# A decoder layer with routed experts on one core: router turned tile by tile, gates of the experts first, last weights in halves, the samples' delta-rule states computed behind the slot indices

## The reference, cut to what matters

```python
def decoder_layer(x, ...):
    h = rmsnorm(x, norm_mix)
    ... = jnp.split(h @ w_in, points, axis=-1)
    # three branches: mLSTM, gated delta rule (state S, 4 heads of 128 x 128 per sequence), cross-attention
    mixed = (sigmoid(gate_a) * (h_a @ w_br_mlstm) + sigmoid(gate_b) * (h_b @ w_br_gdn)
             + sigmoid(gate_c) * (h_c @ w_br_xattn))
    x = x + mixed @ w_out
    x = x + hier_moe(rmsnorm(x, norm_ffn), ...)     # then one final rmsnorm
def hier_moe(h, ...):
    lg = t @ w_router_group + b                     # 4 groups, the best one
    le = t @ w_router_expert + b                    # the best 2 of its 4 experts
    for gidx in range(4):                           # 16 experts, 1024 -> 512 -> 1024
        a = einsum('td,edf->tef', t, w_exp_gate[e0:e1])
        u = einsum('td,edf->tef', t, w_exp_up[e0:e1])
        out = out + einsum('tef,efd->td', silu(a) * u * comb, w_exp_down[e0:e1])
# delta rule, per chunk: Sm = g_last * Sm + k_dec^T v_new     (returned as gdn_S_sample for the samples)
```

## Time and profile before

| | |
|---|---|
| three runs, median (lowest to highest) | 919.81 us (917.28 to 924.47) |
| the profiled execution, whole | 914.95 us |
| its span, first to last instruction | 913.1 us |
| PE busy | 774.1 us (85%), mean granted clock 0.922 |
| DVE, ACT, POOL busy | 278.2, 151.4, 64.1 us |
| moved by DMA | 189.90 MB, mean 208 GB/s |

### The profile page before, as it was taken

How to read it: one execution, slowest core, us unless ns; L and a number is a source line. 1 busy time by engine, 2 the same in 40 slices (tenths; PEclk the granted TensorE clock), 3 DMA queues, 4 the chain that set the end, 5 groups by cost and what they waited for, 6 DMA issues and landing times. The chain is left out here.

```text
span 913.1 us, 10617 instructions
## 1 busy us (share of the span) xinstructions
PE 774.1 (85%) x4441; PEld 421.5 (46%) x4441; DVE 278.2 (30%) x702; ACT 151.4 (17%) x347; POOL 64.1 (7%) x97
## 2 busy tenths in 40 slices
PE   7999999889884989998897899999799787877760
PEld 3544577654552566555654435455333332332220
DVE  2150134568262442164216441135111110110004
ACT  3112122102331301140113110120000000000012
POOL 3102000003111000000001010002100000000002
PEclk9999999889997799999998879999899989988985
DMA  8956525505624200042204337409599999999934
GB/s 275 345 155 198 155 92 184 196 24 180 265 77 176 73 1 1 1 167 110 93 1 144 122 122 276 185 26 412 184 413 423 425 422 418 427 421 421 420 133 155
DMA packets 48830, 189.90 MB, mean 208 GB/s; under 512 B 5110, under 2 KB 5347, under 8 KB 44682
## 3 DMA queue, kind: packets, MB, share of 16 engines
q1 hardware_dynamic: 38922, 155.54, 43.8%
q0 software_dynamic: 9856, 33.63, 11.1%
HBM read 175.47 MB, written 17.88 MB: 212 GB/s over the span
## 5 line engine op out<-in xcount | busy, mean ns | idle before, releaser
L1148 PE MATMUL PS<-ring,arena 128*64 128x512 f32 x384 | 93.1, 643 | 20.8 <-issue 20.8
L1446 ACT ACTIVATE arena<-PS 128x512 f32<-128x512 f32 (+7 forms) x142 | 58.9, 441 | 268.5 <-PE PS L933 73.7
L864 PE MATMUL PS<-ring,hT 128*128 128x512 f32 x192 | 92.5, 630 | 0.4 <-ACT ring L1446 0.4
L562 PE MATMUL PS<-ring,hT 128*128 128x512 f32 x192 | 86.1, 605 | 0.0
L1148 PEld LDWEIGHTS PS<-ring,arena 128*64 128x64 f32 x384 | 32.9, 148 | 80.3 <-issue 80.3
L864 PEld LDWEIGHTS PS<-ring,hT 128*128 128x128 f32 x192 | 37.2, 202 | 43.8 <-issue 43.1
L562 PEld LDWEIGHTS PS<-ring,hT 128*128 128x128 f32 x192 | 36.4, 193 | 45.1 <-issue 45.0
L1446 ACT ACTIVATE brT<-PS 128x256 f32<-128x256 f32 (+2 forms) x39 | 16.3, 418 | 227.2 <-PE PS L1148 191.4
L652 PE MATMUL PS<-hT,ring 128*128 128x288 f32 x192 | 52.5, 431 | 0.0
L2419 DVE SCALAR_TENSOR_TENSOR brT<-brT,PS 128x256 f32<-128x256 f32 x16 | 6.7, 421 | 142.3 <-ACT brT L1446 142.3
L1173 PE MATMUL PS<-ring,brT 128*64 128x512 f32 x192 | 42.5, 594 | 4.6 <-ACT brT L1446 2.6
(11 more groups left out here) (361 smaller groups left out, 913.0 us busy)
## 6 DMA issues: line engine op xcount, KB each, us to landing
ring<-in_w_in SPq DMA_DIRECT2D x15, 2048.0 KB, 10.8
ring<-in_w_exp_gate SPq DMA_DIRECT2D x12, 2048.0 KB, 25.4
ring<-in_w_exp_up SPq DMA_DIRECT2D x12, 2048.0 KB, 24.1
ring<-in_w_exp_down SPq DMA_DIRECT2D x12, 2048.0 KB, 28.5
arena<-in_w_exp_down SPq DMA_DIRECT2D x4, 2048.0 KB, 21.8
arena<-in_w_exp_gate SPq DMA_DIRECT2D x4, 2048.0 KB, 27.7
arena<-in_w_exp_up SPq DMA_DIRECT2D x4, 2048.0 KB, 27.5
moe_in<-in_table SPq DMA_DIRECT2D x2, 2048.0 KB, 13.1
```

The costliest lines, as they stand in the source:

```text
L562: ins = pe.matmul(o[0:n, :], src[:, k, t0:t0 + n], unit(name)[:, 512 * k:512 * k + 512], start=(k == 0), stop=(k == KD - 1))
L864: ins = pe.matmul(PS[:, bg, :], hT[:, k, t0:t0 + n], wg_(k), start=(k == 0), stop=(k == KD - 1))
L1148: ins = pe.matmul(o[64 * hf:64 * hf + 64, :], hg[:, k, 64 * e:64 * e + 64], w[:, :, 512 * k + 256 * hf:512 * k + 256 * hf + 256], start=(k ...
L1446: return act.activation(o, i, f, **kw)
```

## The change

Five edits.

1. The samples' state update (masked values, eight matmuls, 32 block additions, four writes) moves from before `hb` to behind `sid`. Its inputs are kept in unused table columns (`kds`, `vns`), `masked_values` uses part of `brT[2]`; PE uses banks 0 and 4 and one filler matmul a head. POOL writes the heads after its scatters. The load into slots 4/5 now waits for that.
2. The order of pair places becomes 2, 6, 0, 4, the order of pairs gate/up of all four experts first, then the two downs. PE, ACT and DVE follow that order; `actT` has four tiles, so the transposes of one pair stand between other matmuls.
3. The output projections run in the order (0,0) (0,1) (2,0) (2,1) (1,0) (1,1) (tile, half); `x2` itself is transposed, half by half (`x2T`), the norm factor is applied to the logits, and ACT makes `h2p`. Fillers before the logits go, those behind the ranks drop from 12 to 3, 1 a head and 3.
4. The last pair of down weights is loaded in two column halves over both experts, and its results are written in halves by SP. The first reads of slots are issued by SP.
5. The last gathers, additions, norms and writes run in tile order 2, 0, 1.

```diff
-    G_PAIRS = [("gu", 0), ("gu", 1), ("d", 0), ("gu", 2), ("gu", 3), ("d", 1)]
-    PAIR_SLOTS = [4, 2, 6, 0]
+    G_PAIRS = [("gu", 0), ("gu", 1), ("gu", 2), ("gu", 3), ("d", 0), ("d", 1)]
+    PAIR_SLOTS = [2, 6, 0, 4]
...
@@ PE, router
+        turn_mixed(0, 1)
+        project_out(0, 0)
+        turn_mixed(1, 1)
+        turn_mixed(2, 1)
+        project_out(0, 1)
+        project_out(2, 0)
+        project_out(2, 1)
+        turn_x2(0, 0)
+        turn_x2(0, 1)
+        project_out(1, 0)
+        turn_x2(2, 0)
+        turn_x2(2, 1)
...
+        logits(0)
+        project_out(1, 1)
+        turn_x2(1, 0)
+        logits(2)
+        turn_x2(1, 1)
+        logits(1).then_inc(full[1], 1)
         keep_busy(4)
...
-        keep_busy(12)
+        keep_busy(3)
+        for h in range(H):
+            pe.wait_ge(sg("vnb"), h + 1)
+            for g in range(2):
+                bk = (0, 4)[g]
+                o = use(("So2", h, g), bk)
+                pe.matmul(o, kds[:, 128 * h:128 * h + 128],
+                          vnb[h % 2][:, 4 * g:4 * g + 4, :].rearrange("p b v -> p (b v)"),
+                          start=True, stop=True).then_inc(full[bk], 1)
+            keep_busy(1)
+        keep_busy(3)
@@ PE, experts
+            for e in range(EG):
+                gate_up(e, p, g)
+                if e == 1 and g < G - 1:
+                    turn_slots(0, p, g + 1)
+                if e == 2:
+                    turn_act(0, p, g)
+                    turn_act(1, p, g)
+                if e == 3 and g < G - 1:
+                    turn_slots(1, p, g + 1)
+            turn_act(2, p, g)
+            down(0, p, g)
+            turn_act(3, p, g)
+            down(1, p, g)
...
+                if (g, pr_, nn) == (G - 1, 1, 0):
+                    pe.wait_ge(sg("d_half"), 32 * (p + 1))
@@ SP
+                if q == NPAIR - 1:
+                    sp.wait_ge(sg("x_out"), 96 * (p + 1))
+                    for pr_ in range(2):
+                        sp.dma_start(xg[pr_], pair_rows(xrows, pr_, 0)).then_inc(sg(f"xf{pr_}"), 16)
...
                 elif s_ == 4:
-                    sp.wait_ge(*filled(("hbT", 2)))
                     sp.wait_ge(sg("Ss_out"), 16 * H)
                 elif s_ == 6:
-                    sp.wait_ge(*filled((("out", 1), 2)))
+                    sp.wait_ge(*filled((("out", 1), 1)))
...
+            for nn in range(2):
+                sp.wait_ge(*moved("dn", 2 + nn, p, G - 1))
+                sp.dma_start(pair_rows(zrows, 1, G - 1)[:, 512 * nn:512 * nn + 512],
+                             outp[1][:, 512 * nn:512 * nn + 512]).then_inc(sg("z_last"), 16)
@@ POOL
-        for h in range(H):
-            pool.wait_ge(sg("Ssd"), h + 1)
-            pool.dma_start(out["S_s"][0, :, h].rearrange("b k v -> k b v"), Ss[h]).then_inc(sg("Ss_out"), 16)
-        pool.wait_ge(sg("Ss_out"), 16 * H)
...
         pool.wait_ge(sg("sid"), 1)
         scatter_rows()
+        for h in range(H):
+            pool.wait_ge(sg("Ssd"), h + 1)
+            pool.dma_start(out["S_s"][0, :, h].rearrange("b k v -> k b v"), Ss[h]).then_inc(sg("Ss_out"), 16)
@@ DVE
+            ins = stt(LG[0:n, t, :], bank_of("lg")[0:n, 20 * t:20 * t + 20], rst[0:n, t:t + 1], brb[0:n, :],
+                      ALU.mult, ALU.add)
```

More of the change, by code:

```diff
@@ L1085, in keep_busy, with logits @@
+        def logits(t):
+            t0, n = TILES[t]
+            for k in range(KD):
+                if k % 4 == 0:
+                    pe.wait_ge(*taken(("x2T", t, k // 4)))
+                ins = pe.matmul(lg[0:n, 20 * t:20 * t + 20], x2T[:, k, t0:t0 + n], wr[:, k, :],
+                                start=(k == 0), stop=(k == KD - 1))
+            return ins
         def keep_busy(n):
+            pe.wait_ge(free[3], count[3])
             for _ in range(n):
                 pe.matmul(PS[:, 3, :], ident, cst[:, 0:512], start=True, stop=True)
+        turn_mixed(0, 1)
@@ L1410, in slots_group @@
                     read_slots(pr_, p, g + 2)
+            for pr_ in range(2):
+                if (g, pr_) == (G - 1, 1):
+                    continue
                 for nn in range(2):
@@ L1682, in _ @@
                 for h in range(H):
-                    ins = run(vn[0:n, DH * h:DH * h + DH], bank_of("vn2")[n * h:n * h + n, 0:DH], ACT.Copy)
+                    ins = run(vns[:, DH * h:DH * h + DH], bank_of("vn2")[n * h:n * h + n, 0:DH], ACT.Copy)
                 ins.then_inc(freed("vn2"), 1)
@@ L1688, in _ @@
                 ins.then_inc(freed("go2"), 1)
-                for h in range(H):
-                    part_at(t, "vn")
             part_at(t, "hb")
```

409 lines of the change are left out of this document (209 added, 200 removed).

## The result

| | time, us | profiled execution: time / span | granted clock |
|---|---|---|---|
| before | 921.79 (917.28 to 924.47) | 914.95 / 913.1 | 0.922 |
| changed | 910.79 (908.31 to 911.4) | 910.84 / 908.9 | 0.924 |
| changed, timed again beside before (919.46) | 903.94 (900.97 to 911.76) | 902.86 / 901.0 | 0.937 |

The ratio is 0.989, interval 0.985 to 0.993, and in the second timing 0.984 (0.980 to 0.989). So the change makes the kernel about 1.3% faster, 10 to 15 us. The forecast was 21.8 us and 898.0, with a range of 888 to 909: the direction was right, the gain is half to seven tenths of the forecast, and the first measurement lies outside the range (the second, 903.94, inside it).

What follows compares the result with a forecast made beforehand. The prediction took the experts' stage to be bound by weight bytes over DMA. Gains of 13.3 (earlier stream), 7.5 (tail) and 1.0 (last order) made 21.8 us, so 919.81 - 21.8 = 898.0, range 888 to 909.

Steps and rivals of the forecast that it cites:

- What bounds the kernel: Experts' stage: the kernel waits for weight bytes, DMA engines busy all the time at 419 GB/s from 660 to 873 us.
- Part 1: Samples' state update moved away from before the gate projection: 13.2 us of PE time plus 2.4 from a faster projection, 15.6.
- Part 2: Output projections and router: first turned piece to logits takes 42.3 us instead of 46.3, 4.0 us gained.
- Part 3: Indices, scatter, first slots: slots there at 631, first expert matmul at 633 instead of 651.6, 18.6 us earlier.
- no meeting at all: First slots: scatters and slot reads meet no other DMA traffic, so the slots are there at 628.4.
- Part 4: Start of the experts' weight stream: fourth pair issued at 632.5, 21 pairs follow, last byte at 860.0, 13.3 us earlier.
- the 636 that I had named as a sign of being wrong: Fourth pair's issue: later than 636 would show that the state update becomes the path and is longer than before.
- everything in one line: State writes slip behind the weights: 14.4 MB from 601.2, fourth pair issued at 635.5, gain 10.3 instead of 13.3 us.
- Part 5: Tail, last byte to first gather: 10.0 us instead of 17.5, half a down product behind the last byte, gain 7.5.
- End: Last gathers, additions and norms in tile order 2, 0, 1: 1.0 us gained, between a loss of 1 and gain of 2.5.
- Rival 1: State update becomes the path and longer: fourth pair 8.7 us later, gain 13.1, time 906.7; chance 0.22.
- Rivals 2 and 3: Second: faster update, slots, tail, 27 us gained, 893, chance 0.10. Third: PE's low clock bounds experts, about 1010, chance 0.06.

Runs made afterwards that it cites:

- x3: Changed kernel with the samples' state update and its writes put back in their old place, pair places 4, 2, 6, 0; ratio to before 0.998.
- x2: Changed kernel with the samples' state update and its writes left out, twelve fillers on PE in its place; ratio to before 0.976.
- x1: Changed kernel without the four state writes to DRAM, the fourth pair waiting only for the computed states; ratio to before 0.976.
- x8: Changed kernel with pair places 2, 0, 6, 4 and half a pair loaded before the last output projection; ratio to before 0.983.
- z1: Changed kernel with half a pair early, the fourth pair's loads held apart, final norm's gain loaded at the first output projection; ratio to before 0.980.
- z2: Changed kernel with mixT moved, second pair and half a pair loaded early, gain early, fourth pair's loads held apart; ratio to before 0.979.
- x9: Changed kernel with the third pair loaded behind the reads of the first slots; ratio to before 0.990.

## Why the prediction was right and wrong

- **What bounds the kernel.** Right that the experts' stage waits for bytes. Wrong where it begins now: I let the stream start with the fifth pair in before, where the hole does end, and with the fourth in the changed kernel. There the hole is closed, and the line starts at P.
- **Part 1, state update moved, 15.6 us.** Right: x3 shows 16 to 17 in the front. "It delays no matmul" is right for the work on PE and DVE (x2 is no earlier than x1) and wrong for its writes: without them the first expert matmul comes 5.9 us sooner behind P (x1).
- **Part 2, 4.0 us.** The router's span shrank by 5.9 us, better than forecast. It did not matter: slots follow P, not the logits. P itself came 11.5 and 12.9 us earlier in the two profiles (forecast 12.8), and it would have come some 4 us earlier still with the projections in their old order (x3 against before, 4.3; one front and another of the same code differ by up to 2.8).
- **Part 3, slots at 631, gain 18.6.** This step failed. It took 20 us for the two pairs and, for the rest, the middle between one line (633) and no meeting at all (628.4). The slots were to be there 30.8 us behind P (631 - 600.2). They were read at 29.6 and landed only some 8 to 9 us later, since all four state writes were ahead of them; a read in an empty queue took 3.8. The first expert matmul came 41.7 us behind P, forecast 32.8. In the runs with both pairs behind P the slots are read 29.4 to 30.3 us behind it (31.3 in before) whatever the router, DVE or POOL do; with half a pair less it is 24.8, and with a whole pair less 22.0, where POOL's issue takes over. 11.3 MB (two pairs, gain, rows) at 410 GB/s are 27.6 us. Gain in the first matmul, aligned at `w_br_gdn`: 8.5 and 9.5 us.
- **Part 4, the joint, 13.3 us.** This step failed with it. "A state write took 3.8 us" was read in an empty queue; here it is 11.8. The fourth pair went out 38.4 us behind P, forecast 632.5 - 600.2 = 32.3; on the forecast's axis 638.6, later than the 636 that I had named as a sign of being wrong. The case that I had written down and put aside, everything in one line, gave 35.3. A sum of bytes would have shown it: from 600.2 to the last byte at 860.0 I had 109 MB in 259.8 us, 420 GB/s from the first instant, with no latency and no dip. Measured are 265.6 and 266.1 us. With the tail's 1.8 to 3.5 that makes the 8.2 to 9.5 us that are missing behind P. x8 shows the cause: bytes taken out of the line move slots, fourth pair and end, though no wait of the fourth pair was changed. The Trainium skill, DMA: Bandwidth & Descriptors, section Queues, rings and completion order, has the engines take turns between queues; I had drawn from it that POOL's small writes pass the weights. The trace does not bear that reading out: the six scatters landed in 12.0 us in the median beside the pairs, and when the slots could be read, 29.6 us at some 400 GB/s had moved the bytes of the pairs and the gain as well. Nor did the rows that I had quoted for it. In before the pairs of 612.97 and 614.00 and the gain are 8.9 MB and were through near 636.5 (an estimate, at 410 GB/s), so the scatters from 633.21 on met them for only some 3 of their 11.0 us.
- **Part 5, tail, 7.5 us (10.0 left of 17.5).** Missed by its size, 4.0 and 5.7 came: last byte (near 874 and 867.8) to first gather 13.5 us in the first profile and 11.8 in the second, against 17.5 before. The halves gave nothing, since two down products in a row stand on PE there and not half a one.
- **End, 1.0 us.** Right: 21.4 us from gather to end against 22.3. Whether it is the order of the tiles, no run shows.
- **Rivals.** Rival 1 had the number (906.7, between the two measurements) and the sign of the late fourth pair, by luck, for its cause was another: the update was shorter than before (13.7 us), the queue was longer. Rivals 2 and 3 did not come: from 660 to 866 us the granted clock is 0.94, and most expert products take 7.09 us, some 8.78 to 9.84, with waits of up to 4.0 us in front of them.

The sum as it came out: 11.5 to 13 us ahead of P; behind it 6.3 MB more (15 us), the hole of before closed (about 10), tail and end 5 to 6.5 better: nothing.

## What to carry to other kernels

Before an edit is priced where a stream begins, add up the bytes from the point at which the DMA engines become full to the last byte and divide by the rate: no rearrangement behind that point can beat this, and a transfer's latency read in an idle queue is not valid inside it. Moving work from PE to "behind the stream's start" is a trade of PE time for DMA time if it holds a buffer or writes results; price both. What helps is to move bytes ahead of that point, into an idle stretch, until the queue runs dry again (x8 and z1 help, z2 hardly more than z1).

## What the runs showed of the hardware

- Loads of the last pair in column halves run slower than whole ones. x6, last two pairs halved: 384 to 389 GB/s between 850 and 864 us; x5, whole: 408 to 412 in the same stretch (2 us windows). Half a row is 2 KB, a whole one 4 KB. The changed kernel, with only its last pair in halves, shows the same in its last windows (385 to 388 from 862 to 872 us). That eats part of what halves bring.
- POOL's issue of an indirect DMA takes 0.87 to 1.05 us without the state update on DVE (x2) and 1.35, 1.67 and 1.73 us where a multiplication of two operands in SBUF (L2439, 1.21 us) runs beside it. Beside the additions (L2449), of which one operand comes from PSUM, it stays at 0.89 to 1.01. In x9 such a multiplication meets the fifth scatter and not the fourth, and it is the fifth that takes 1.54 us, the fourth 0.97. The Trainium skill, GPSIMD Engine Reference, section Key points, says that its SBUF interfaces are shared with VectorE when that has two SBUF inputs; the trace agrees (these rows), and here it cost no time.
- The same down product behind the same wait of 2.9 us took 7.09, 8.78, 9.96 or 10.02 us in different executions. Which one it is, no run here shows.
